# A two-block transformer kernel on one core: first weights by halves, narrower waits, held-back gate products, a new order at the last layer's passage, later POOL passes

## What is computed

```python
def reference(...):                       # cut
    h = x                                 # [512, 1024]
    for i in range(2):                    # first block
        m = even_mixer(h) if i == 0 else odd_mixer(h)
        h = layer_norm(ALPHA * h + m, ln_g[i, 0], ln_b[i, 0])                              # norm "m0", "m1"
        h = layer_norm(ALPHA * h + memory_cross_attention(h, mem), ln_g[i, 1], ln_b[i, 1])  # "a0", "a1"
        h = layer_norm(ALPHA * h + square(relu(h @ w1)) @ w2, ln_g[i, 2], ln_b[i, 2])       # "f0", "f1"
    n = rms_norm(h, norm_gain)            # second block
    ya = diff_attention(q, k, v, lam) * silu(g_a)         # branch a: softmax pair, p0 - lam * p1
    yb = sliding_window_attention(q, k, v, sinks) * silu(g_b)
    yc = forgetting_attention(q, k, v, logf) * silu(g_c)
    merged = sum(gate_b * (y_b @ w_up_b) for b in "abc")  # three 1024-wide gates from n
    return rms_norm(h + merged @ w_o, final_gain)
```

## Time and profile before

| | us |
|---|---|
| median of 3 runs | 2294.74 (2294.55 to 2296.74) |
| the profiled execution, its own time | 2293.56 |
| its span, first to last instruction | 2291.7 |
| PE busy | 2238.5 (98%) |
| DVE busy | 1273.0 (56%) |
| ACT busy | 924.2 (40%) |
| POOL busy | 164.4 (7%) |
| chain that ended last | PE 88%, DVE 7%, ACT 3% |

### The profile page before, as it was taken

One profiled execution on the slowest core, in us unless ns is written; L12 is line 12 of the kernel. 1 busy time (PEld: TensorE's weight loads), 2 busy tenths in 40 slices (PEclk: granted clock), 3 DMA queues, 4 the chain that ended last, 5 costly groups with the idle time before them and its releaser, 6 DMA issues.

```text
span 2291.7 us, 27734 instructions
## 1 busy us (share of the span) xinstructions
PE 2238.5 (98%) x11201; PEld 1841.4 (80%) x11201; DVE 1273.0 (56%) x1886; ACT 924.2 (40%) x1690; POOL 164.4 (7%) x149
## 2 busy tenths in 40 slices
PE   8999999999999999999999999999989999999998
PEld 6886888878788888888887788888867688887777
DVE  5999887745733434735574573333452843642664
ACT  3253764343422323345434232232253534533453
POOL 1110000210400000400022040000000000000000
PEclk9999999999999999999999999999999999999999
DMA  5352245323333232321152223323233132123113
GB/s 172 104 156 74 74 133 193 116 92 128 104 111 95 97 103 92 121 74 56 62 187 84 66 93 112 109 92 92 92 115 106 37 92 74 56 92 92 55 38 119
DMA packets 181588, 226.95 MB, mean 99 GB/s; under 512 B 17587, under 2 KB 140214, under 8 KB 180438
## 3 DMA queue, kind: packets, MB, share of 16 engines
q1 hardware_dynamic: 169686, 192.23, 26.6%
q10 hardware_dynamic: 9664, 22.33, 2.8%
q0 software_dynamic: 2112, 10.64, 1.4%
HBM read 213.78 MB, written 9.18 MB: 97 GB/s over the span
## 4 chain that ended last, share of the span: by engine, by line
PE 88%; DVE 7%; ACT 3%; issue 1%; DMA 0%; ACTq 0%; DVEq 0%; SPq 0%
PE gemm L657 26%; PE gemm L659 26%; PE gemm L658 26%; PE aux L790 2%; DVE w_lo L2323 1%; PE aux L1047 1%; PE aux L1069 1%; DVE x_lo L2346 1%; DVE work L2461 1%; PE aux L1425 1%; PE gemm L966 1%; ACT w_hi L1480 1%; PE aux L1411 1%; DVE mxs L3037 1%; PE aux L1380 1%
## 5 line engine op out<-in xcount | busy, mean ns | idle before, releaser
L657 PE MATMUL gemm<-x_hi,w_hi 128*128 128x512 f32 x1288 | 515.9, 401 | 12.3 <-DVE x_lo L2346 6.4
L658 PE MATMUL gemm<-x_lo,w_hi 128*128 128x512 f32 x1288 | 503.1, 391 | 0.0
L659 PE MATMUL gemm<-x_hi,w_lo 128*128 128x512 f32 x1288 | 503.1, 391 | 0.0
L2323 DVE TENSOR_TENSOR w_lo<-raw,w_hi 128x1024 fp32r<-128x1024 f32 x222 | 284.2, 1304 | 270.6 <-ACT w_hi L1480 269.7
L1480 ACT ACTIVATE w_hi<-raw 128x1024 fp32r<-128x1024 f32 x222 | 228.1, 1053 | 271.2 <-PE gemm L659 246.8
L657 PE MATMUL gemm<-w_hi,y_hi 128*128 128x512 f32 (+1 forms) x832 | 321.6, 386 | 1.3 <-DVE h L2410 1.3
L658 PE MATMUL gemm<-w_lo,y_hi 128*128 128x512 f32 (+1 forms) x832 | 317.0, 381 | 0.0
L657 PEld LDWEIGHTS gemm<-x_hi,w_hi 128*128 128x128 f32 x1288 | 242.8, 189 | 82.7 <-issue 18.2
L2319 DVE TENSOR_TENSOR w_lo<-raw,w_hi 128x1024 fp32r<-128x1024 f32 x140 | 168.2, 1221 | 252.8 <-ACT w_hi L1478 243.6
L659 PE MATMUL gemm<-w_hi,y_lo 128*128 128x512 f32 x768 | 298.9, 389 | 0.0
L659 PEld LDWEIGHTS gemm<-x_hi,w_lo 128*128 128x128 f32 x1288 | 242.6, 188 | 51.6
(11 more groups left out here) (345 smaller groups left out, 2817.1 us busy)
## 6 DMA issues: line engine op xcount, KB each, us to landing
raw<-in_mlp_w_dram SPq DMA_DIRECT2D x64, 1024.0 KB, 5.4
raw<-in_w_in_dram SPq DMA_DIRECT2D x31, 1024.0 KB, 5.2
raw<-in_odd_w_in_dram SPq DMA_DIRECT2D x12, 1024.0 KB, 5.3
raw<-in_even_w_in_dram SPq DMA_DIRECT2D x10, 1024.0 KB, 5.2
raw<-in_even_w_in_dram SPq DMA_DIRECT2D x16, 512.0 KB, 5.2
raw<-in_xa_w_k_dram SPq DMA_DIRECT2D x8, 1024.0 KB, 5.2
raw<-in_xa_w_v_dram SPq DMA_DIRECT2D x8, 1024.0 KB, 5.2
raw<-in_even_w_out_dram SPq DMA_DIRECT2D x8, 1024.0 KB, 5.1
```

The lines of the kernel that those rows point to most:

```text
L657: pe.matmul(dst, a_hi, b_hi, start=first, stop=False)
L658: pe.matmul(dst, a_hi, b_lo, start=False, stop=False)
L659: return pe.matmul(dst, a_lo, b_hi, start=False, stop=last)
L2323: dve.tensor_tensor(w_lo[:, s % W_SLOTS, :, :], raw[:, s // 2 % RAW_SLOTS, :, half], w_hi[:, s % W_SLOTS, :, :].bitcast(F32), ALU.subtract)\
```

## The change

Eight edits, in order of time. SP issues the first panel's two halves apart: the first at once, the second when x and the first half have landed; ACT and DVE split one piece ahead of the last columns of x and the second behind them. POOL's passes of a0 and a1 wait until chunk 2 of the MLP has been read. The small rows stand ahead of the last panel of `gla_qk`, their copy behind chunk 5's. At the passage DVE's splits stand elsewhere, PE turns tiles 2 and 3 a product earlier, and the first two pieces of `qk_a` stand ahead of lambda. In branch a, ACT does a due gate chunk before the unit's exponentials. In all branches at most 60 gate products stand between the units, 62 ahead of the output's turns, and 2 behind them. The scores wait for the last chunk of qk_a, kv_b and v_c. DVE scales the whole third row tile of the output.

```diff
--- before.py
+++ after.py
@@ -533,5 +533,14 @@
 
-            load(0)
+            def load_first(half):
+
+                col = half * D
+                sp.dma_start(raw[:, 0, :, half * P:half * P + P],
+                             w["even_w_in"][0:D, col:col + P].rearrange("(k p) n -> p k n", p=P))\
+                  .then_inc(raw_loaded[0], 16)
+
+            load_first(0)
             for t in range(TT):
                 sp.wait_ge(x_loaded[t], 16)
+            sp.wait_ge(raw_loaded[0], 16)
+            load_first(1)
             load(1)
@@ -547,3 +556,3 @@
             for t in range(TT):
-                sp.wait_ge(S["out_first"], t + 1)
+                sp.wait_ge(S["out_first"], t + 1 if t < TT - 2 else t)
                 sp.wait_ge(S["out_second"], t + 1)
@@ -602,2 +611,4 @@
                 wait_aux(pool, ("turn", name, KC - 1))
+                if name in ("a0", "a1"):
+                    chunk_read(pool, stage_chunk("mlp" + name[1]) + 2)
                 for t in range(TT):
@@ -1110,4 +1121,5 @@
             filled_norm("f0", h, "xv1a", 2)
-            gemm("gla_qk", x_hi, x_lo, wide="chunks", **row_fill("f0", h))
+            gemm("gla_qk", x_hi, x_lo, panels=3, wide="chunks", **row_fill("f0", h))
             small_rows("glow", 1, 16)
+            gemm("gla_qk", x_hi, x_lo, panels=1)
 
@@ -1273,3 +1285,3 @@
                         scores(us[n + 2])
-                    gate_products(b, gate_steps(b, n, len(us)))
+                    gate_products(b, min(gate_steps(b, n, len(us)), KC * KC - 4))
                     for g in range(2 if b == "c" else 1):
@@ -1278,5 +1290,3 @@
                     after(u)
-                gate_products(b, KC * KC)
-                at["gate"] = 0
-                at["panel"] += 4
+                gate_products(b, KC * KC - 2)
 
@@ -1289,2 +1299,5 @@
                     ins.then_inc(aux_done, 1)
+                gate_products(b, KC * KC)
+                at["gate"] = 0
+                at["panel"] += 4
                 gemm(f"up_{b}", y_hi, y_lo, ready=lambda k: aux_read(pe, name, k))
@@ -1317,3 +1330,3 @@
                             ins.then_inc(pieces_used, 1)
-                        if k == 5 and t + 1 < TT:
+                        if k == (5 if t == 0 else 4) and t + 1 < TT:
                             turn_tokens(t + 1)
@@ -1325,3 +1338,3 @@
             gemm_rows("g_a", x_hi, x_lo, halves=1)
-            chunk_read(pe, stage_end_chunk("g_a") - 1)
+            chunk_read(pe, stage_end_chunk("qk_a") - 1)
 
@@ -1354,3 +1367,3 @@
             gemm_rows("g_b", x_hi, x_lo, halves=1)
-            chunk_read(pe, stage_end_chunk("g_b") - 1)
+            chunk_read(pe, stage_end_chunk("kv_b") - 1)
 
@@ -1397,3 +1410,3 @@
             gemm_rows("g_c", x_hi, x_lo, halves=1)
-            chunk_read(pe, stage_end_chunk("g_c") - 1)
+            chunk_read(pe, stage_end_chunk("v_c") - 1)
             pe.wait_ge(S["log_ready"], GH + 1)
@@ -1462,3 +1475,3 @@
                     n = s // 2
-                    act.wait_ge(raw_loaded[n % RAW_SLOTS], raw_value(n))
+                    act.wait_ge(raw_loaded[n % RAW_SLOTS], 16 if s == 0 else raw_value(n))
                     if s >= W_SLOTS:
@@ -1643,3 +1656,3 @@
                     if t == TT - 1 and i == 0:
-                        split_to(0)
+                        split_chunk()
                     bank = wait_aux(act, ("x", t, i))
@@ -1998,4 +2011,5 @@
                                           scale=128.0 ** -0.5 if j < 4 else 1.0), c)
-            bank = wait_aux(act, ("glow",))
-            free_aux(act.activation(GL[0:32, :], bank[0:32, :], ACT.Copy), ("glow",))
+                if j == 5:
+                    bank = wait_aux(act, ("glow",))
+                    free_aux(act.activation(GL[0:32, :], bank[0:32, :], ACT.Copy), ("glow",))
 
@@ -2127,4 +2141,4 @@
                     token_operand(0)
-                if t == TT - 1:
                     split_chunk()
+                if t == TT - 1:
                     token_operand(1)
@@ -2258,5 +2272,8 @@
                         square_unit(n - 1)
+                    if b == "a":
+                        gate_rows(gate_steps(b, n, len(us)) // KC)
                     if n + AHEAD[b] < len(us):
                         exps(us[n + AHEAD[b]])
-                    gate_rows(gate_steps(b, n, len(us)) // KC)
+                    if b != "a":
+                        gate_rows(min(gate_steps(b, n, len(us)) // KC, KC - 1))
                 if b == "a":
@@ -2265,3 +2282,2 @@
                     act.activation(sm[:, 9, :], sm[:, 9, :], ACT.Exp, scale=-0.5).then_inc(S["ya_rstd"], 1)
-                gate_rows(KC)
                 for j in range(4):
@@ -2269,2 +2285,3 @@
                     operand_hi(y_hi[:, j, :], bank[:, :], y_hi_done, lam[:, 3:4] if b == "a" else 1.0)
+                gate_rows(KC)
                 split_chunks(2 * first + W_SLOTS + KC)
@@ -2297,6 +2314,7 @@
                            .then_inc(S["out_rstd"], 1)
-                        act.wait_ge(S["out_rstd"], t + 1)
-                        act.wait_ge(S["gained"], t + 1)
-                        act.activation(OUT[:, t, 0:512], OUT[:, t, 0:512], ACT.Identity, scale=rstd[:, 0, t:t + 1])\
-                           .then_inc(S["out_first"], 1)
+                        if t != TT - 2:
+                            act.wait_ge(S["out_rstd"], t + 1)
+                            act.wait_ge(S["gained"], t + 1)
+                            act.activation(OUT[:, t, 0:512], OUT[:, t, 0:512], ACT.Identity,
+                                           scale=rstd[:, 0, t:t + 1]).then_inc(S["out_first"], 1)
 
@@ -2825,3 +2843,3 @@
 
-            def token_rest(t):
+            def token_rest(t, beside=lambda: None):
 
@@ -2838,2 +2856,3 @@
                     free_aux(ins, key)
+                    beside()
 
@@ -2842,7 +2861,5 @@
                 if t == TT - 1:
-                    split_chunk()
-                    token_rest(0)
+                    token_rest(0, split_chunk)
                     split_chunk()
                 if t == TT:
-                    split_chunk()
                     token_rest(1)
@@ -2861,2 +2878,3 @@
                     token_rest(3)
+                    split_to(FIRST_PANEL["qk_a"])
 
@@ -3200,3 +3218,5 @@
                         dve.wait_ge(S["out_rstd"], t)
-                        dve.tensor_scalar(OUT[:, t - 1, 512:D], OUT[:, t - 1, 512:D], rstd[:, 0, t - 1:t], None,
+                        dve.wait_ge(S["gained"], t)
+                        cols = slice(0 if t == TT - 1 else 512, D)
+                        dve.tensor_scalar(OUT[:, t - 1, cols], OUT[:, t - 1, cols], rstd[:, 0, t - 1:t], None,
                                           ALU.mult).then_inc(S["out_second"], 1)
```

## The result

The changed kernel takes **2278.74 us** (median of 4 runs, 2277.67 to 2280.97) against 2294.81 of the kernel before in the same comparison: ratio 0.9929, interval 0.9912 to 0.9947. A second comparison gave 2279.52 against 2296.58, ratio 0.9922 (0.9909 to 0.9935). The forecast was 2279.0, in a range of 2274.0 to 2287.5. That the sum fits so well is partly luck, since errors cancel: the start was put too high, POOL's part too low, and the clock's part came elsewhere than forecast.

A forecast was written before the change was run, and what follows sets the result against it. TensorE (PE) was taken as the bound, busy 2238.5 of 2291.7 us, leaving 53 us idle plus slow-clock cost; gains summed to 15.7 us, giving 2277.9 from 2293.56, or 2279.0 as a median, range 2274 to 2287.5.

The forecast's parts named there:

- 1 start, idle time: At the start, half the first panel ahead of x's last columns lets PE begin earlier: 2.4 us, bounds 1.06 and 4.06.
- 2 POOL (a0, a1): In both MLPs, POOL's later gain and bias stop slowing DVE's splits that PE waits for: 3.2 us, bounds 0 and 3.2.
- 3 small rows: Ahead of the last gla_qk panel, the small rows' copy is hidden behind 48 matmuls or more: 0.7 us.
- 4 passage: From f1 to v_a, the wait before qk_a goes (2.61) and token tiles shift (1.1): 3.7 us, bounds 1.5 and 8.0.
- 5 branch a: In branch a, ACT's gate chunk before exponentials brings turned copies earlier: 1.6 us, bounds 0 and 3.6.
- 8 tail: At the tail, row 2's output scaling moves from ACT to DVE: 0.3 us, bounds -0.3 and 0.7.
- clock, terms 1 and 5: Slow-clock stretches at the start and at 1835.93 in branch a go: 1.7 us each, bounds 0 and 1.7 each.
- A: Rival: DVE starves PE beside the moved POOL work, so the POOL gain is 0: 2282.2 us, chance 0.12.
- B: Rival: slow-clock stretches stay at the start and in branch a, perhaps a third at v_a: 2282.4 to 2284.1, chance 0.20.
- C: Rival: ACT and DVE bound the passage and branch a, so removed waits come back: 2286.0 us, chance 0.15.
- D: Rival: the scores' narrower waits gain nothing, as PE's next wait ends unchanged: 2280.0 us, inside the forecast's 0.44.
- E: Rival: POOL's rows of h come too late for the MLP residual adds, so slower: 2300 us, chance 0.03.

The follow-up runs named there:

- u_order: The change with ACT's gate chunks behind the exponentials in branch a again; median 2279.44 us.
- v_final: The change with gate products held back in b alone, first piece split ahead of x's second tile, mem requested after the parameters; median 2275.36 us.
- v_pass: The change with the second token tile's rest ahead of row tile 2's norm on DVE and PE's turns of the third tile later; median 2281.97 us.

## Why the prediction came out as it did

Term by term, by the steps of the prediction:

| term | predicted | measured |
|---|---|---|
| 1 start, idle time | 2.4 | 1.6 at equal clock |
| 2 POOL (a0, a1) | 3.2 | 4.7 |
| 3 small rows | 0.7 | 0.7 |
| 4 passage | 3.7 | 3.3 to 4.0 |
| 5 branch a | 1.6 | 1.5 |
| 6 held-back products | -0.6 | -0.5 |
| 7 narrower waits | 1.0 | 0.9 to 1.2 |
| 8 tail | 0.3 | 0.3 |
| sum without the clock | 12.3 | 12.5 to 13.5 |
| clock, terms 1 and 5 | 3.4 | 2.6 to 4.6, a remainder, and not where expected |

Term 3 is the section between the 776th and 1821st group, 701.46 against 700.80; it was not tried by itself. Term 8 is from the last group's start to the end of the span, 8.40 against 8.08, not tried either. The clock's row is what the other terms leave of the difference of the medians (16.1 and 17.1); it was not measured by itself. Two slow stretches fewer (4 and 6 in the old order, 2.9 in the mean in the new), at 1.5 each, would make 3.

**Term 1 failed at its cover.** "SP now holds panel 1, `w_small` and the parameters behind that wait; panel 1 is wanted only after two chunks" weighed panel 1 and forgot when the parameters are wanted. Their last DMA is issued at 23.1 instead of 20.3, PE goes on at 27.2, and it has stood 1.75 for them (0.9 in three other traces). The first gemm itself came at 14.3 to 15.2 (14.4 forecast): in the first trace ACT's split starts at 12.05, behind the third tile's casts, and DVE's `w_lo` at 13.14 is ahead of the last `x_lo` at 14.28.

**Term 2 was too small**: it left out an `x_lo` wait of 0.5 in a0, and took a stall for its idle time alone. Three restarts at 0.3 and this 0.5 make 1.4 of the 1.5. The cover held, with 0.1 us a chunk to spare instead of 0.2.

**The clock was right in sum and wrong in place.** I expected the slow stretches at the start and in branch a's end to go. The second went in all 12 traces, but also in the one where the wait that I tied it to is back (u_order). The first went in half. One at a1's entry came in. That the mean clock rose is measured: 0.992 to 0.996 in the executions before, 0.995 to 0.999 in the change's. A slow stretch cost 1.5 in branch c (97.15 and 97.13 against 95.62 us) and 1.5 at the start (13.4 us from the first gemm to the 17th group with one, 11.86 in v_final, which has neither a slow stretch nor a wait there), near my 1.7. Where PE would wait anyway it cost less: 0 to 0.7 at the passage, and 0.5 in the change's start, where full clock leaves 12.95 us with the wait of 0.9 for the parameters. Why branch a's slow stretch is gone stays open, and so does the one at a1.

**The rivals.** A (DVE starves PE) is refuted by the empty waits behind 594. B holds for single executions only: the first trace kept its slow stretches at the start and had five in all, but that execution took 2280.97, below B's 2282.4. C is wrong: the gains at the passage and in branch a stay to the end. In v_pass its mechanism seems to show: one step further the waits come back on the same chain. D was right for a's narrow wait alone, as forecast. E is refuted: POOL ended at 621.8, 14 us ahead of the first residual add at 635.65.

The prediction stood better for the branches (terms 5 to 7, replayed on paper operation by operation) than for the DMA queue at the start, where no such replay was made.

## What to carry to other kernels

Find each PE stall's last link, and price an edit at the stall plus some 0.3 us for the restart; but replay the engine that takes the moved work, the queue that issues DMAs included, up to the next thing that is wanted from it. Compare sections between two equal instructions in two traces, not totals, when single executions differ by as much as the edit is worth. A load that nothing wants yet (mem here) is best asked for last: with it on its way the issue of those behind it took longer.
